# The shared expert in plain fp32, held in one slot of the experts' ring and spread between the routing's steps, in a one-layer hybrid block on one core

## The reference

```python
def moe(h, ...):
    s = sigmoid(t @ w_router)                      # 384 x 64
    # groups of 8 experts, best 4 groups, best 8 experts of them per token
    wk = s[idx] / sum(s[idx]) * ROUTED_SCALE
    act = silu(t @ w_gate_e) * (t @ w_up_e) * gates        # 64 experts, width 256
    routed = act @ w_down_e
    shared = (silu(t @ w_gate_s) * (t @ w_up_s)) @ w_down_s   # width 256, every token
    return routed + shared
```

## Time and profile before

| | us |
|---|---|
| median of 3 runs (lowest, highest) | 1068.91 (1066.82, 1069.91) |
| the profiled execution's own time | 1072.45 |
| its span, first to last instruction | 1070.7 |
| PE busy | 894.3 (84%) |
| DVE, ACT, POOL busy | 348.4, 258.6, 161.0 |
| DMA traffic over the span | 299.57 MB |
| mean granted TensorE clock, share of full | 0.919 |

### The profile page before, as it was taken

How to read it: one execution, slowest core, us unless ns; L and a number is a source line. 1 busy time by engine, 2 the same in 40 slices (tenths; PEclk the granted TensorE clock), 3 DMA queues, 4 the chain that set the end, 5 groups by cost and what they waited for, 6 DMA issues and landing times.

```text
span 1070.7 us, 12051 instructions
## 1 busy us (share of the span) xinstructions
PE 894.3 (84%) x4264; PEld 536.3 (50%) x4264; DVE 348.4 (33%) x835; ACT 258.6 (24%) x423; POOL 161.0 (15%) x212
## 2 busy tenths in 40 slices
PE   4799899999899895898868878878878989878860
PEld 2478686888898894443323323333333334333320
DVE  1634553666465667111111111111111111111105
ACT  2456424433333331111111011111111111111111
POOL 6200000000000412021011111111011011112112
PEclk9799899999999987999889899889989989989985
DMA  9965776222233415989999999999999999989914
GB/s 347 349 219 192 251 259 156 70 68 69 79 118 125 182 68 207 412 285 386 393 403 392 375 390 379 374 391 363 359 381 353 366 354 389 388 351 396 338 33 180
DMA packets 90474, 299.57 MB, mean 280 GB/s; under 512 B 18372, under 2 KB 40960, under 8 KB 65600
## 3 DMA queue, kind: packets, MB, share of 16 engines
q1 hardware_dynamic: 67600, 263.21, 62.7%
q0 software_dynamic: 14128, 31.27, 10.9%
q10 hardware_dynamic: 8704, 4.54, 1.7%
HBM read 287.16 MB, written 29.63 MB: 296 GB/s over the span
## 4 chain that ended last, share of the span: by engine, by line
PE 53%; DMA 34%; DVE 6%; ACT 2%; issue 2%; POOL 1%; SPq 1%; ACTq 1%; POOLq 0%; DVEq 0%
DMA gu<-in_w_up_e_dram 30%; PE bank L1296 18%; PE bank L962 7%; PE bank L964 7%; PE bank L963 7%; PE bank L1316 4%; PE bank L990 2%; DMA xg<-h_dram,slot_tok 2%; PE bank L1125 1%; PE bank L1031 1%; PE bank L1283 1%; DMA chunk_raw<-in_w_ada_dram 1%; DMA y_dram<-y_sb,slot_row 1%; PE bank L1057 1%; PE bank L1103 1%
## 5 line engine op out<-in xcount | busy, mean ns | idle before, releaser
L1296 PE MATMUL bank<-gu,x_t 128*64 128x512 f32 (+1 forms) x1024 | 322.0, 677 | 87.6 <-DMA gu<-in_w_up_e_dram 86.5
L1296 PEld LDWEIGHTS bank<-gu,x_t 128*64 128x64 f32 (+1 forms) x1024 | 114.3, 168 | 263.7 <-issue 243.9
L1316 PE MATMUL bank<-dn,a_t 128*64 128x512 f32 (+1 forms) x512 | 145.8, 598 | 1.2 <-ACT y_sb L927 1.2
L647 POOL DMA_INDIRECT y_dram<-y_sb,slot_row x40 | 64.0, 1600 | 488.2 <-issue 337.4
L1712 DVE TENSOR_TENSOR act_sb<-silu_sb,bank 128x256 f32<-128x256 f32 x40 | 16.8, 421 | 367.4 <-ACT silu_sb L936 367.4
L936 ACT ACTIVATE silu_sb<-bank 128x256 f32<-128x256 f32 x40 | 15.4, 385 | 369.8 <-PE bank L1296 369.8
L962 PE MATMUL bank<-h_hi,chunk_lo 128*128 128x384 f32 x272 | 96.0, 353 | 0.0
L964 PE MATMUL bank<-h_hi,chunk_hi 128*128 128x384 f32 x272 | 92.4, 340 | 0.0
L963 PE MATMUL bank<-h_lo,chunk_hi 128*128 128x384 f32 x272 | 92.1, 339 | 0.0
L1316 PEld LDWEIGHTS bank<-dn,a_t 128*64 128x64 f32 (+1 forms) x512 | 48.9, 151 | 69.6 <-issue 68.2
L927 ACT ACTIVATE y_sb<-bank,slot_gate 128x512 f32<-128x512 f32 x80 | 50.6, 684 | 124.4 <-PE bank L1316 110.8
(11 more groups left out here) (319 smaller groups left out, 1035.8 us busy)
## 6 DMA issues: line engine op xcount, KB each, us to landing
gu<-in_w_gate_e_dram SPq DMA_DIRECT2D x64, 1024.0 KB, 10.7
gu<-in_w_up_e_dram SPq DMA_DIRECT2D x64, 1024.0 KB, 22.4
dn<-in_w_down_e_dram SPq DMA_DIRECT2D x64, 1024.0 KB, 22.5
chunk_raw<-in_w_ada_dram SPq DMA_DIRECT2D x24, 1024.0 KB, 8.8
chunk_raw<-in_w_in_dram SPq DMA_DIRECT2D x18, 1024.0 KB, 5.4
chunk_raw<-in_w_out_dram SPq DMA_DIRECT2D x4, 1024.0 KB, 4.9
chunk_raw<-in_w_pa_dram SPq DMA_DIRECT2D x2, 1024.0 KB, 5.0
chunk_raw<-in_w_pb_dram SPq DMA_DIRECT2D x2, 1024.0 KB, 5.1
```

What stands on the lines that cost most here:

```text
L647: pool.indirect_dma_start(y_dram[:, :], bass.IndirectOffsetOnAxis(ap=slot_row[:, u % UN:u % UN + 1], axis=0), y_sb[u % 2][:, :], None, bou ...
L1296: mm = pe.matmul(bank[2 + u % 2][at_x, :].rearrange("p (g n) -> p g n", g=2), x_t[:, cols], wide[:, :, k, :], start=(k == 0), stop=(k == K ...
L1316: mm = pe.matmul(bank[5 + half][at_x, :], a_t[:, cols], dn[x % RING][:, wc], start=(k == 0), stop=(k == 1))
```

## The change

The shared expert is no longer split. Its three matrices go, as they are, into slot 3 of the experts' ring (`shared_gu`, `shared_dn`), loaded when attention is done, and its products are plain fp32, one token tile at a time with gate and up side by side, like a block of an expert (`shared_gate_up`, `shared_turn_act`, `shared_down`). Its 24 gate and up products are spread between the routing's steps on PE; its down products come after block 2's row numbers and before block 0. Experts 0 to 2 load when the output products are done, expert 3's gate and up behind the third shared tile, its down weights behind expert 5's gate and up in SP's queue, after the shared down products.

Norm and router go by tiles: `xhat2` of a tile is written as soon as its rstd is there, ScalarE makes half of the blocks of h2, and PE interleaves the transposes with the router. A sigmoid of one column stands ahead of the squares. Ranks come out with the experts on the partitions, so they need no transposes, with a mark (MARK, 4096) for a token's own choice. The two tables are looked up apart: with the ranks alone VectorE makes the token numbers of blocks 0 and 1 (`early_rows` with two columns), and the gates follow (the other six columns). The zeros for `y_dram` are written when the mixer is done; the shared rows are stored by POOL behind block 2's gather.

```diff
-        xg = [at(f"xg{i}", [P, D], EX + 48 + 4 * i) for i in range(2)]
-        act_sb = at("act_sb", [P, FE], EX + 56)
-        silu_sb = at("silu_sb", [P, FE], EX + 57)
-        ring = [EX + 60, EX + 84, EX, EX + 24]
+        xg = [at(f"xg{i}", [P, D], 12 + 4 * i) for i in range(2)]
+        act_sb = at("act_sb", [P, FE], 20)
+        silu_sb = at("silu_sb", [P, FE], 21)
+        ring = [EX + 84, EX, EX + 24, EX + 60]
+        shared_gu = at("shared_gu", [P, 4096], ring[3])
+        shared_dn = at("shared_dn", [P, 2048], ring[3] + 16)
...
+        shared_sb = at("shared_sb", [P, TT, D], EX + 150.5)
         x_t = at("x_t", [P, KD * CAP], EX + 108)
+        zeros = at("zeros", [P, D], EX + 108)
+        a_sh = at("a_sh", [P, TT, 2 * CAP], EX + 112)
...
+                    if x == RING - 1:
+                        sp.wait_ge(S["shd_mm"], TT)
...
-            for x in range(FIXED):
-                if x == 0:
-                    sp.wait_ge(S["o_evac"], NSTEP)
-                if x == 1:
-                    sp.wait_ge(S["sh_mm"], 4)
-                if x == 2:
-                    sp.wait_ge(S["shd_mm"], 6)
+            sp.wait_ge(S["o_evac"], NSTEP)
+            for g, w in enumerate((w_gate_s, w_up_s)):
+                sp.dma_start(shared_gu[:, 2048 * g:2048 * g + 2048], w[0].rearrange("(p k) n -> p (k n)", k=KD)).then_inc(S["shared_loaded"], 16)
+            sp.dma_start(shared_dn[:, :], w_down_s[0].rearrange("(p k) n -> p (k n)", k=2)).then_inc(S["shared_loaded"], 16)
+            sp.wait_ge(S["out_mm"], 12)
+            for x in range(FIXED - 1):
                 load_gu(x, None, slice(x, x + 1))
                 load_dn(x, None, slice(x, x + 1))
+            sp.wait_ge(S["sh_mm"], TT)
+            load_gu(FIXED - 1, None, slice(FIXED - 1, FIXED))
             sp.wait_ge(S["passes_ready"], 1)
             passes = sp.value_load(more_i[0:1, 0:1], min_val=0, max_val=MAXPASS - 1) + 1
-            late = []
+            late = [(FIXED - 1, slice(FIXED - 1, FIXED))]
...
+            pool.memset(zeros[:, :], 0.0).then_inc(S["zeros_made"], 1)
+            pool.wait_ge(S["zeros_made"], 1)
+            for t in range(TT):
+                pool.dma_start(y_dram[NTOK + t * P:NTOK + (t + 1) * P, :], zeros[:, :]).then_inc(S["b_zero"], 16)
...
+                    if first and u == 0:
+                        for t in range(TT):
+                            pool.wait_ge(S["shd_evac"], 2 * t + 2)
+                            pool.dma_start(y_dram[t * P:(t + 1) * P, :], shared_sb[:, t, :]).then_inc(S["added"], 16)
...
-            squares(1, xhat2, S["sumsq2"])
...
-                split_high(act, n)
...
-                act.activation(h2_hi[:, :, t * P:(t + 1) * P], h2_t[:, :, t * P:(t + 1) * P], ACT.Copy).then_inc(S["h2_high"], 1)
+            act.activation(fold_junk[:, :], quarter[:, 0:1], ACT.Sigmoid)
+            for t in range(TT):
+                act.wait_ge(S["out_done"], 10 + t)
+                act.activation(xhat2[:, t, :], x_sb[:, t, :], ACT.Square, scale=D ** -0.5,
+                               accum_out=sumsq[:, 1, t:t + 1]).then_inc(S["sumsq2"], 1)
+            act.wait_ge(S["scale2_ready"], 1)
+            for t in range(TT):
+                cond = int(t > 0)
+                act.wait_ge(S["xt2"], 2 * t + 2)
+                for k in range(4, KD):
+                    ins = act.activation(h2_t[:, k, t * P:(t + 1) * P], bank[4 + (2 * t + 1) % 4][:, (k % 4) * P:(k % 4 + 1) * P],
+                                         ACT.Identity, scale=scale2[:, k, cond:cond + 1], bias=mod_t[:, 3, k, cond:cond + 1])
+                ins.then_inc(S["h2_act"], 1)
...
-            split_high(act, number[("sd", 0)])
...
-            act.activation(hs_hi[:, :, :], hs_t[:, :, :], ACT.Copy).then_inc(S["hs_high"], 1)
+            def shared_silu(t):
+                act.wait_ge(S["sh_mm"], t + 1)
+                if t:
+                    act.wait_ge(S["sh_act"], t)
+                act.activation(silu_sb[:, :], bank[2 + t % 2][:, 0:FE], ACT.Silu).then_inc(S["sh_silu"], 1)
+            def shared_out(t):
+                act.wait_ge(S["shd_mm"], t + 1)
+                for half in range(2):
+                    act.activation(shared_sb[:, t, 512 * half:512 * half + 512], bank[5 + half][:, :],
+                                   ACT.Copy).then_inc(S["shd_evac"], 1)
+            act.wait_ge(S["rank_mm"], 1)
+            act.activation(rank_et[:, :], bank[1][0:NE, 0:NTOK], ACT.Copy).then_inc(S["sides_evac"], 1)
             act.wait_ge(S["kv_stored"], 32)
...
+            shared_silu(0)
+            act.wait_ge(S["sides_mm"], 1)
+            act.activation(gate_et[:, :], bank[6][0:NE, 0:NTOK], ACT.Copy).then_inc(S["sides_evac"], 1)
+            shared_silu(1)
+            shared_silu(2)
+            act.wait_ge(S["h2_stored"], 16 * TT)
...
+            turn_rows2(0)
+            turn_rows2(1)
+            pe.wait_ge(S["router_loaded"], 16)
+            route(0)
+            turn_rows2(2)
+            route(1)
+            route(2).then_inc(S["router_mm"], 1)
...
-            pe.wait_ge(S["h2_split"], TT)
-            for m in range(4):
...
-                    mm = three_products(bank[2 + m][:, 0:NTOK], [a[:, at_m:at_m + P] for a in w],
...
+            def shared_gate_up(t, ks):
+                wide = shared_gu[:, :].rearrange("p (g k n) -> p g k n", g=2, n=FE)
+                for k in ks:
+                    mm = pe.matmul(bank[2 + t % 2][:, :].rearrange("p (g n) -> p g n", g=2), h2_t[:, k, t * P:(t + 1) * P],
+                                   wide[:, :, k, :], start=(k == 0), stop=(k == KD - 1))
+                    if k == KD - 1:
+                        mm.then_inc(S["sh_mm"], 1)
+            def shared_turn_act(t):
+                pe.wait_ge(S["sh_act"], t + 1)
+                if t:
+                    pe.wait_ge(S["sh_at"], t)
+                for k in range(2):
+                    mm = pe.transpose(bank[4][:, k * P:(k + 1) * P], act_sb[:, k:FE:2], ident[:, :])
+                mm.then_inc(S["sh_at_mm"], 1)
+            def shared_down(t):
+                pe.wait_ge(S["sh_at"], t + 1)
+                if t:
+                    pe.wait_ge(S["shd_evac"], 2 * t)
+                for half in range(2):
+                    for k in range(2):
+                        mm = pe.matmul(bank[5 + half][:, :], a_sh[:, t, k * CAP:(k + 1) * CAP],
+                                       shared_dn[:, k * D + 512 * half:k * D + 512 * half + 512], start=(k == 0), stop=(k == 1))
+                mm.then_inc(S["shd_mm"], 1)
+            def early_rows(n, cols):
+                for t in range(TT):
+                    mm = pe.matmul(bank[7][:, cols], onehot[n][:, t, :], row_tab[:, n, t, cols], start=(t == 0), stop=(t == TT - 1))
+                return mm
+            def side_values(out, table):
+                for t in range(TT):
+                    mm = pe.matmul(out[:, t * NSIDE:(t + 1) * NSIDE], table[:, t * P:(t + 1) * P], side_pick[:, :], start=True, stop=True)
+                return mm
+            pe.wait_ge(S["shared_loaded"], 48)
+            shared_gate_up(0, range(0, 5))
+            pe.wait_ge(S["chosen_ready"], 1)
+            pe.wait_ge(S["tables_made"], 3)
             pe.wait_ge(S["score_done"], 1)
+            for t in range(TT):
+                for j in range(t + 1):
+                    pe.matmul(bank[1][0:NE, t * P:(t + 1) * P], chosen_b[:, j, :], (ones_b if j < t else order_b)[:, :],
+                              start=(j == 0), stop=(j == t))
+            for j in range(TT):
+                pe.matmul(bank[0][0:NE, 0:NE], ones_b[:, 0:NE], chosen_b[:, j, :], start=(j == 0), stop=(j == TT - 1))
+            for j in range(TT):
+                mm = pe.matmul(bank[0][0:NE, NE:NE + 1], chosen_b[:, j, :], ones_b[:, 0:1], start=(j == 0), stop=(j == TT - 1))
+            mm.then_inc(S["rank_mm"], 1)
+            shared_gate_up(0, range(5, KD))
+            pe.wait_ge(S["picks_made"], 1)
+            pe.wait_ge(S["sides_evac"], 1)
+            side_values(bank[1], rank_et).then_inc(S["sorted_mm"], 1)
+            shared_gate_up(1, range(0, 2))
+            pe.wait_ge(S["h2r_evac"], 6)
             for n in range(2):
...
+                pe.wait_ge(S["onehot_ready"], n + 1)
+                if n:
+                    pe.wait_ge(S["idx_ready"], 2)
+                early_rows(n, slice(0, 2)).then_inc(S["idx_mm"], 1)
+                shared_gate_up(1, range(2 + 2 * n, 4 + 2 * n))
+            pe.wait_ge(S["gates_made"], 1)
+            for t in range(TT):
+                mm = pe.transpose(bank[6][0:NE, t * P:(t + 1) * P], gates[:, t, :], ident[:, :])
+            mm.then_inc(S["sides_mm"], 1)
+            shared_gate_up(1, range(6, KD))
+            pe.wait_ge(S["picks_made"], 3)
             pe.wait_ge(S["sides_evac"], 2)
...
+            side_values(bank[0], gate_et)
             pe.matmul(bank[0][0:1, 384:384 + NE], expert_no[:, :], seq_pick[:, :], start=True, stop=True)
...
```

(84 more changed lines are left out.)

245 lines of the change are left out of this document (74 added, 171 removed).

## The result

The changed kernel takes 1056.87 us (median of 4 runs, 1053.31 to 1057.77) against 1069.41 us for the kernel before in the same runs: ratio 0.9873, interval 0.9855 to 0.9891. Two repeats beside other kernels gave 0.9891 (0.9861 to 0.9921) and 0.9906 (0.9885 to 0.9927). On the 1068.91 us of before these are 1055.3, 1057.3 and 1058.9. The change is worth 11.8 us by their mean, 0.9890, where 8.8 was forecast: the direction held, and the gain was sized 3 us too small.

A forecast was written before the change was run, and what follows sets the result against it. PE paces the first four expert blocks, then the weight stream. Block 0 starting 4.2 us earlier plus 4.6 from block 2's gather make 8.8 us, so 1068.91 becomes 1060.1 us, range 1056.0 to 1066.5.

The forecast's parts named there:

- The end moves one for one with block 3's gate and up: Expert loop: later weight loads hang on the slot released there, so the end gains the same 8.8 us.
- The rival of a backlog that holds the end: Weight stream: an unseen backlog sets the end, nothing is carried over, time stays 1068.9 us; chance 0.08.
- Router, 3.0 us: Norm and router by tiles: last router product ends at 374.5 instead of 377.5, 3.0 us earlier.
- From the router to block 0, 49.2 us: PE's queue from router's end to block 0's gate and up: summed to 49.2 us, before 50.5.
- the 24 transposes: PE, after the router: 4.8 us, paced by ScalarE's copies as before.
- The half rate on the gate and up products: Shared gate and up on PE: a clock dip covers 2.4 us of them, costing 1.2 more (0 to 4).
- New waits: PE before block 0: row numbers 0.8, shared tile 2's turn 0.7, pass count read 0.9; together 2.4 us (0 to 4).
- Small products: PE between router and block 0: ranks, side tables, expert order, row numbers and nine transposes, together 5.1 us.
- Block 2's gather, 4.6 us: Block 2's start: its rows, gathered earlier with no expert loads in flight, arrive in time, removing a 4.6 us delay.
- The bound on VectorE: Tables for later passes precede shared tile 2's copy; half a microsecond is free, each one beyond costs PE one.
- The rival of fewer waits: PE before block 0: clock stays full, added waits are hidden, 3.6 us more gain: 12.4 in all, 1056.5 us; chance 0.12.
- the slower one: Shared fp32 gate and up products all at half rate: 19.7 us more, less 8.8, giving 1079.8 us; chance 0.08.

The follow-up runs named there:

- the dip filled in both kernels: Products that nobody reads put into PE's gaps ahead of the router: ratio 0.9857 in the changed kernel, 0.9977 in the kernel before.
- the run with the order alone: The kernel before with only block 2's gather issued ahead of the shared rows' three stores in GpSimd's queue: ratio 0.9964, 3.9 us faster.

## Why the prediction was right in its mechanism and short in its size

The step that failed is the time from the router to block 0. The forecast gave it 1.2 us of gain (50.5 to 49.2) and it was 3.65 by the means; the router was put 0.6 too high, and the gather's stall 0.8 too low. Together these are 2.6 of the 3 us that are missing.

**The end moves one for one with block 3's gate and up.** Right: over executions in which that point moves by 21 us, the rest takes 597 us, 2 more or less. The rival of a backlog that holds the end, whatever block 3 does, fell.

**Router, 3.0 us.** Measured 1.7 against the trace that I had and 2.4 over the means. The order of work was as laid out; tile 2's transposes took 1.91 and the last two tiles 4.41 us where I had 1.0 and 3.8, a part of them at the half rate, which I had allowed for only in the last tile. Against the trace that I had, the changed kernel without its dip would gain 14.95 - 11.79 = 3.2. With the dip filled in both kernels it is 13.64 - 11.79 = 1.85, so the new order of work by itself is worth less than the 3.0.

**From the router to block 0, 49.2 us: the step that failed.** It took 46.6. Term by term: the 24 transposes 3.6 (370.96 to 374.57) where the sum had 4.8 "paced by ScalarE's copies as before". They had been paced by the clock, 0.50 over nearly all of them, and at 1.00 the copies cost them only 0.25 and 0.35. The half rate on the gate and up products, 1.2, didn't come. New waits 0.88 + 0.79 = 1.67, not 2.4: the read of the pass count is hidden. Small products some 0.7 more than 5.1. Gate and up 20.8, down 10.3, two waits 2.60 and block 0's 1.87 are as summed. The differences, -1.2 - 1.2 - 0.7 + 0.7 and 0.1 less on gate and up, make 2.5 of the 2.6.

**Block 2's gather, 4.6 us.** Right in kind and for that trace: 24.95 against 20.37. It was 6.15 in the second execution of before, which adds to the mean. But the stall isn't all wait. PE's row that waits for the gather, in the first and in the second trace of before, and a window of the first:

```profile
446.84 1.97 PE L1283 MATMUL bank<-ident,xg 128*128 128x128 f32 x8 [2.98 <-DMA xg<-h_dram,slot_tok]
```

```profile
449.23 1.97 PE L1283 MATMUL bank<-ident,xg 128*128 128x128 f32 x8 [3.08 <-DMA xg<-h_dram,slot_tok]
```

```profile
447.00:448.00 1.00, 1.00 (x6) 0.50 1.05 430
```

So only 3.0 of the 4.6 us are the gather. The rest is half rate behind the wait: the granted clock is 0.50 from 446.3 to 449.7 in the first trace and from 448.4 to 455.0 in the second, which is where its stall is 1.6 us longer. That the stores ahead of it in its own queue make the gather late is shown by the run with the order alone.

**The bound on VectorE.** "Half a microsecond is free" came out as 1.4, and the danger that I named is real: in the run without down products it took 7 of the 10 us, and the half rate behind it 2.25 more.

**The sum.** 8.8 against 10.1 in the profiled pair. Most of the other 1.7 us of the measured 11.8 (1.4, by the means above) belong to the execution that I summed against: its dip at the router began late, and the half rate behind its stall was the shorter one. That rests on two traces of before and three of after. The rival of fewer waits had the direction of the miss, and half of its 3.6 us; the slower one, half rate over the shared products, fell: in all three traces of the changed kernel router to block 0 takes 46.6 us at a granted clock of 1.00.

## What to carry to other kernels

When a queue of work is summed from a trace, look up the granted clock under each row that gives a duration: a pace that was read as another engine's was here half the clock, and one execution shows only one of the places where the dip can fall. A stall costs more than its wait: the 3 us for the gather were followed by a half rate that cost 1.6 us in one trace and 3.1 in the other. Before an engine's work is taken out, find what runs beside it: 10 us of products were worth nothing while VectorE's tables stood beside them. And a transfer on the path should stand ahead of bulk stores in its own queue, above all when other queues are busy.

## What was unexpected

The half rate came behind gaps of 0.5 to 2.5 us in PE's work and could be kept away with 2 us of products that nobody reads; a gap of 6.11 us cost the next block 2.25 us. The three stores of 0.5 MB ahead of a gather cost it 1.3 us on idle DMA engines and 9 us on busy ones. And the start of the kernel, untouched, differs by 5 us between executions, and the granted clock from 20 to 60 us with it, which is nearly half of what the change is worth.
